# Neighbourhood attention with stacked query halves, three score buffers, and turning ahead of the last values

## The reference, cut to what matters

```python
def dense_attention(q, k, v):
    s = jnp.einsum('bqhd,bkhd->bhqk', q, k).astype(jnp.float32) * (q.shape[-1] ** -0.5)
    p = jax.nn.softmax(s, axis=-1).astype(v.dtype)
    return jnp.einsum('bhqk,bkhd->bqhd', p, v)

def neighbourhood_attention(q, k, v, k_ctx, v_ctx, rpb, rows):
    ...
    s_loc = jnp.einsum('brqhd,brikhd->bhrqik', qg, k_band).astype(jnp.float32) * scale + bias.astype(jnp.float32)
    s_loc = jnp.where(in_win[:, None, :], s_loc, -jnp.inf)
    s_loc = s_loc.reshape(bsz, h, rows, GRID_W, wr * GRID_W)
    s_ctx = jnp.einsum('brqhd,blhd->bhrql', qg, k_ctx).astype(jnp.float32) * scale
    p = jax.nn.softmax(jnp.concatenate([s_loc, s_ctx], axis=-1), axis=-1).astype(v.dtype)
    ...
    o = jnp.einsum('bhrqik,brikhd->brqhd', p_loc, v_band) + jnp.einsum('bhrql,blhd->brqhd', p_ctx, v_ctx)
    return o.reshape(bsz, n, h * dh)

def diff_attend(q1, q2, k1, k2, v, lam):
    ...
    p = jax.nn.softmax(s1, axis=-1) - lam * jax.nn.softmax(s2, axis=-1)
    return jnp.einsum('bhqk,bkhd->bqhd', p.astype(v.dtype), v)
```

## Time and profile before

| | |
|---|---|
| median of 3 runs | 2925.27 us (2922.05 to 2929.17) |
| the profiled execution | 2929.45 us, of which the span is 2927.6 us |
| TensorE matmul busy | 2836.5 us, 97% of the span |
| VectorE busy | 1750.9 us, 60% |
| ScalarE busy | 990.6 us, 34% |
| mean granted TensorE clock | 0.988 of full speed |

### The profile page before, as it was taken

One profiled execution on the slowest core, in us unless ns is written; L12 is line 12 of the kernel. 1 busy time (PEld: TensorE's weight loads), 2 busy tenths in 40 slices (PEclk: granted clock), 3 DMA queues, 4 the chain that ended last, 5 costly groups with the idle time before them and its releaser, 6 DMA issues.

```text
span 2927.6 us, 37226 instructions
## 1 busy us (share of the span) xinstructions
PE 2836.5 (97%) x15519; PEld 2435.8 (83%) x15519; DVE 1750.9 (60%) x2406; ACT 990.6 (34%) x1371; POOL 121.5 (4%) x157
## 2 busy tenths in 40 slices
PE   6999999999999999999989999999999988999999
PEld 5888887979788888789878888888888987888887
DVE  6656655555567777566486565655555348454454
ACT  4333333232333222332275232222213237432222
POOL 0100000000001100000000000000000000000000
PEclk9999999999999999999989999999999999999999
DMA  7343344545234644333600212333322151222232
GB/s 248 121 139 108 119 153 149 175 119 168 92 117 141 179 144 146 97 123 101 144 30 16 86 58 87 94 105 92 99 65 92 61 116 39 64 85 89 93 108 72
DMA packets 267507, 317.17 MB, mean 108 GB/s; under 512 B 24859, under 2 KB 236203, under 8 KB 267340
## 3 DMA queue, kind: packets, MB, share of 16 engines
q1 hardware_dynamic: 240764, 230.60, 25.8%
q0 software_dynamic: 19456, 72.00, 8.3%
q10 hardware_dynamic: 7120, 12.20, 1.3%
HBM read 291.96 MB, written 11.27 MB: 104 GB/s over the span
## 4 chain that ended last, share of the span: by engine, by line
PE 89%; DVE 5%; ACT 2%; DVEq 2%; issue 1%; DMA 0%; ACTq 0%
PE psum L625 26%; PE psum L627 26%; PE psum L626 26%; PE psum L1068 2%; PE psum L855 1%; PE psum L1080 1%; DVE dneg L2473 1%; DVE sba L2484 1%; DVE n_t L1921 1%; PE psum L842 1%; ACT pt L1738 1%; PE psum L928 1%; DVE w_lo L1933 1%; PE psum L1159 1%; PE psum L1149 0%
## 5 line engine op out<-in xcount | busy, mean ns | idle before, releaser
L625 PE MATMUL psum<-hs_hi,w_hi 128*128 128x512 f32 x1632 | 647.2, 397 | 10.4 <-DVE hs_lo L1925 7.6
L1933 DVE TENSOR_TENSOR w_lo<-raw,w_hi 128x2048 fp32r<-128x2048 f32 (+1 forms) x246 | 435.7, 1771 | 357.8 <-ACT w_hi L1301 245.7
L626 PE MATMUL psum<-hs_hi,w_lo 128*128 128x512 f32 x1632 | 637.3, 391 | 0.0
L627 PE MATMUL psum<-hs_lo,w_hi 128*128 128x512 f32 x1632 | 637.3, 390 | 0.0
L625 PEld LDWEIGHTS psum<-hs_hi,w_hi 128*128 128x128 f32 x1632 | 307.6, 188 | 84.5 <-issue 10.2
L627 PEld LDWEIGHTS psum<-hs_lo,w_hi 128*128 128x128 f32 x1632 | 307.2, 188 | 65.1
L626 PEld LDWEIGHTS psum<-hs_hi,w_lo 128*128 128x128 f32 x1632 | 307.7, 189 | 61.3 <-issue 1.0
L1993 DVE SCALAR_TENSOR_TENSOR ada_acc<-ada_raw,csil,ada_acc 128x512 f32<-128x512 f32 x392 | 279.7, 749 | 38.0 <-DMA ada_raw<-in_w_ada 19.8
L1311 ACT CAST w_hi<-raw 128x2048 fp32r<-128x2048 f32 (+1 forms) x138 | 191.3, 1386 | 325.7 <-PE psum L627 313.8
L625 PE MATMUL psum<-mid_hi,w_hi 128*128 128x512 f32 x768 | 300.7, 392 | 0.0
L626 PE MATMUL psum<-mid_hi,w_lo 128*128 128x512 f32 x768 | 299.1, 389 | 0.0
(11 more groups left out here) (361 smaller groups left out, 4534.2 us busy)
## 6 DMA issues: line engine op xcount, KB each, us to landing
raw<-in_w_in SPq DMA_DIRECT2D x56, 1024.0 KB, 5.2
ada_raw<-in_ada_w POOLq DMA_DIRECT2D x96, 512.0 KB, 4.0
raw<-in_w_ff SPq DMA_DIRECT2D x48, 1024.0 KB, 5.5
raw<-in_w_ff SPq DMA_DIRECT2D x96, 512.0 KB, 3.4
ada_raw<-in_w_ada POOLq DMA_DIRECT2D x32, 512.0 KB, 4.1
raw<-in_w_in SPq DMA_DIRECT2D x24, 512.0 KB, 4.6
raw<-in_w_ret_out SPq DMA_DIRECT2D x16, 512.0 KB, 3.4
raw<-in_w_out SPq DMA_DIRECT2D x8, 1024.0 KB, 5.0
```

The costliest lines, as they stand in the source:

```text
L625: pe.matmul(dst, lhi, rhi, start=start, stop=False)
L626: pe.matmul(dst, llo, rhi, start=False, stop=False)
L627: return pe.matmul(dst, lhi, rlo, start=False, stop=stop)
L1933: low = dve.tensor_tensor(w_lo[par][:, k0:kt], raw[par][:, k0:kt], w_hi[par][:, k0:kt].bitcast(F32), ALU.subtract)
```

## The change

**Scores by two products.** A head fills only half of the 128 rows, so the queries' high half now lies in one half of `naqs` and the low half in the other, and the keys' high half stands twice, one above the other (`naks_hi`), as does the low half (`naks_lo`). One matmul against `naks_hi` gives high by high plus low by high; a second against `naks_lo` gives high by low plus low by low. The stacked keys are made by 16 DMAs from SBUF to SBUF in each layer.

**Buffers.** Three score buffers of two banks (`SPAIR`) in place of two of three, four buffers of exponentials (`sba`, `sbb`), two of turned tiles (`pt2`).

**Orders.** The two attentions get a TensorE loop of their own, and the copy of a full item's turned tiles is split into tiles 4 and 5, then 0 to 3. Some jobs of ScalarE and VectorE move from the end of the differential loop into it.

```diff
+                def stack_keys(tokens, context, src, src_c, made):
+                    for dst_of, whole, j in ((tokens, src, 1), (context, src_c, 2)):
+                        sp.wait_ge(made, 2 * l + j)
+                        for a in range(2):
+                            for half in range(2):
+                                sp.dma_start(dst_of(a)[HD * half:HD * (half + 1)].bitcast(F32),
+                                             whole[HD * a:HD * (a + 1)].bitcast(F32)).then_inc(nk_stacked, 16)
+                stack_keys(lambda a: naks_hi[:, a:4:2, :], lambda a: nakcs_hi[:, a:4:2, :], nak_hi, nakc_hi, nk_hi)
+                stack_keys(lambda a: naks_lo[:, a:4:2, :], lambda a: nakcs_lo[a], nak_lo, nakc_lo, nk_split)
                 sp.wait_ge(df_s, 24 if l == 0 else 40)
...
+            def diff_attention(l, score, free, next_score):
...
                     if i + 2 < len(its):
                         score(i + 2, its[i + 2])
+                    elif i < len(its):
+                        next_score(i + 2 - len(its))
...
+            def na_attention(l, score):
...
+                t0 = turn_groups(att_items(0)[0], 24) * l
+                score(2, its[2])
+                for i in range(len(its) + 1):
+                    if i < len(its):
+                        it = its[i]
+                        pe.wait_ge(na_exp, i0 + i + 1)
+                        if i == 0:
+                            pe.wait_ge(df_out, g0 + its[-1].group + 1)
+                            pe.wait_ge(df_pt, i0 + len(its))
+                        else:
+                            pe.wait_ge(na_pt, t0 + turn_groups(its, i))
+                        if it.pos == 1 and it.group and not it.ctx:
+                            pe.wait_ge(na_out, g0 + it.group)
+                        for tiles in ([range(2)] if it.ctx else [range(4, 6), range(4)]):
+                            for t in tiles:
+                                mm = pe.transpose(T2[:, t * P:(t + 1) * P], sbn[i % 4][:, t * P:(t + 1) * P], ident[:])
+                            mm.then_inc(na_t, 1)
+                    if i:
+                        last = its[i - 1]
+                        pe.wait_ge(na_pt, t0 + turn_groups(its, i) + (1 if i < len(its) and not its[i].ctx else 0))
+                        if last.pos == 0 and last.group:
+                            pe.wait_ge(na_out, g0 + last.group)
+                        item_values(last, pt2[(i - 1) % 2], nav).then_inc(na_pv, 1)
+                    if i + 3 < len(its):
+                        score(i + 3, its[i + 3])
...
                 def na_score(i, it):
...
+                    dst = SPAIR[i % 3]
...
+                    if i == 0:
+                        pe.wait_ge(nk_stacked, 256 * (l + 1))
+                    if i < 3:
+                        pe.wait_ge(df_e2, i0 + len(its) - (1 if i == 0 else 0))
                     else:
+                        pe.wait_ge(na_exp, i0 + i - 2)
...
+                        pe.matmul(dst[:, 0:S], q_, naks_hi[:, it.head, :], start=True, stop=False)
+                        pe.matmul(dst[:, 0:S], q_, naks_lo[:, it.head, :], start=False, stop=True)
                     a_ = 0 if it.ctx else S
+                    pe.matmul(dst[:, a_:a_ + SC], q_, nakcs_hi[:, it.head, :], start=True, stop=False)
+                    pe.matmul(dst[:, a_:a_ + SC], q_, nakcs_lo[it.head % 2][:, it.head // 2, :], start=False, stop=True).then_inc(na_s, 1)
...
+                def na_take_pt(i, it):
+                    if i >= 2:
+                        act.wait_ge(na_pv, i0 + i - 1)
+                    elif i == 0:
+                        act.wait_ge(df_pv, i0 + N_)
+                    for j, (t_, n_) in enumerate([(0, 2)] if it.ctx else [(4, 2), (0, 4)]):
+                        act.wait_ge(na_t, t0 + turn_groups(its, i) + j + 1)
+                        turned(i % 2, t_, n_).then_inc(na_pt, 1)
...
-                    if 4 <= i < 8:
-                        odd = i % 2
-                        z = (qz_hi if i < 6 else qz_lo)[odd][HD * (1 - odd):HD * (2 - odd)]
-                        act.activation(z, zero_c(HD * (1 - odd)), ACT.Copy, scale=0.0)
-                    if i == N_ - 4:
+                    if i == N_ - 9:
                         act.copy(nak_hi[:], nak[:]).then_inc(nk_hi, 1)
...
+                    elif i == N_ - 8:
                         act.copy(nakc_hi[:], nakc[:]).then_inc(nk_hi, 1)
+                    elif i == N_ - 6:
+                        nq_his(first_of[0])
...
                 na_exps(0, its[0])
+                na_exps(1, its[1])
                 for i in range(N_):
-                    if i + 1 < N_:
-                        na_exps(i + 1, its[i + 1])
+                    if i + 2 < N_:
+                        na_exps(i + 2, its[i + 2])
...
-                    take_pt(i, its[i], na_t, na_pt, na_pv)
+                    na_take_pt(i, its[i])
...
+                    if i == N_ - 8:
+                        key_los(1, nak_lo, nak, nak_hi)
+                    elif i == N_ - 7:
+                        key_los(2, nakc_lo, nakc, nakc_hi)
+                    elif i == N_ - 5:
+                        nq_los(first_of[0])
+                    elif i == N_ - 4:
+                        dve.wait_ge(bb_in, 128 * (l + 1))
+                        mask_bias(0)
...
+                na_max(0, its[0])
                 df_take(its[-1])
                 na_max(1, its[1])
+                na_max(2, its[2])
...
-                    if i + 2 < N_:
-
-                        if its[i + 2].pos == 0 and not its[i + 2].ctx:
-                            mask_bias(its[i + 2].head)
-                        dve.wait_ge(na_exp, i0 + i + 1)
-                        na_max(i + 2, its[i + 2])
+                    if i + 3 < N_:
+
+                        if its[i + 3].pos == 0 and not its[i + 3].ctx:
+                            mask_bias(its[i + 3].head)
+                        na_max(i + 3, its[i + 3])
```

More of the change, by code:

```diff
@@ L150, in att_items, with turn_groups @@
     return its, 24 * l, 8 * l
+def turn_groups(its, i):
+    return sum(1 if it.ctx else 2 for it in its[:i])
 def build(nc, d, out):
@@ L1047, in _, with item_values @@
             feed_forward(FU["ff"], 0, 2, 0, (hs_ready, lambda k: 8 + k + 1), None, "", ahead=context_tiles, twin=True)
-            def attention(l, kind, sems, score, values, free, last_copied):
-                done_t, pt_ok, p_ok, pv, outs = sems
+            def item_values(it, pt_, values):
+                nt = it.keys // P
+                for t in range(nt):
+                    mm = pe.matmul(O2[:, it.pos * HD:(it.pos + 1) * HD], pt_[:, t, :],
+                                   values[:, t + 6 - nt, it.head * HD:(it.head + 1) * HD], start=t == 0, stop=t == nt - 1)
+                return mm
+            def diff_attention(l, score, free, next_score):
                 its, i0, g0 = att_items(l)
@@ L1192, in _ @@
                 its = att_items(l)[0]
-                groups = its[-1].group + 1
                 def df_free(it):
@@ L1199, in df_free @@
                         pe.wait_ge(df_out, g0 + it.group)
-                def na_free(it):
-                    pe.wait_ge(df_out, g0 + groups)
-                    if g0 + it.group:
-                        pe.wait_ge(na_out, g0 + it.group)
-                attention(l, "diff", (df_t, df_pt, df_comb, df_pv, df_out), df_score, dfv, df_free, lambda: None)
                 def na_score(i, it):
-                    c = it.head // 2
                     tok = slice(it.tile * P, (it.tile + 1) * P)
-                    dst = S3[i % 2]
+                    dst = SPAIR[i % 3]
@@ L1227, in _ @@
+                diff_attention(l, df_score, df_free, lambda i: na_score(i, its[i]))
+                na_attention(l, na_score)
                 y0 = 12 * l
@@ L1783, in na_exps @@
-                    if it.pos == 0 and it.group > 1:
-                        act.wait_ge(na_out, g0 + it.group - 1)
-                    act.activation(sba[i % 2][:, 0:it.keys], S3[i % 2][:, 0:it.keys], ACT.Exp, bias=stat2[:, i % 2:i % 2 + 1],
-                                   accum_out=den[:, it.group % 2, it.pos:it.pos + 1]).then_inc(na_exp, 1)
+                    if i >= 4:
+                        act.wait_ge(na_t, t0 + turn_groups(its, i - 3))
+                    if it.pos == 0 and it.group > 3:
+                        act.wait_ge(na_out, g0 + it.group - 3)
```

145 lines of the change are left out of this document (66 added, 79 removed).

## The result

The changed kernel takes 3030.87 us (median of 6 runs, 3025.86 to 3040.03) against 2928.29 us for the kernel before (median of 6 runs). The ratio is 1.036, with an interval of 1.034 to 1.037: 3.6% slower. The forecast of 3006 us has the direction and the cause. It is 25 us short. The largest part of that is one term of the sum, the clock; the jobs moved into the differential loop are the second.

The account below looks back on a forecast made before the run. TensorE was taken to bound the kernel before, a closed ring the changed loop. 2929.45 us + 58 (26 + 24 + 6 + 2) + 23 for the clock = 3010, less 4.2 to the median: 3006 us; range 2976 to 3041.

Parts of the forecast that it names:

- The closed ring (part 2): Neighbourhood loop: values wait behind a newer item's score, maximum and exponential; one item per turn, 5.58 us against 3.11.
- Start and end (parts 3 and 4): Neighbourhood stretches: first values 8.0 us after the last differential values; whole stretches +24 us in layer 0, +26 in layer 1.
- The clock (part 7): Neighbourhood loop: TensorE's clock goes to and fro, 40% at the half clock, 23 us more.
- The sum: Whole kernel: 2929.45 us profiled + 58 at the full clock + 23 for the clock = 3010 us.
- the half clock throughout: Rival: TensorE stays at 1.2 GHz in the neighbourhood stretches, 58 us for the clock, 3041 us; chance 0.15.
- the likeliest case: Mixture of full and half clock in the neighbourhood stretches, 2992 to 3024 us; chance 0.56.
- Part 1: Neighbourhood scores: two products for three remove TensorE work, 11.5 us over full items and 1 us over context items.
- the rival of an open ring: Neighbourhood loop: ScalarE's first copy precedes the wait for the exponential, period 2.75 us, 2913 us in all; chance 0.05.
- The moved jobs (part 5): Differential loop: key and query low halves and first mask, moved inside on nearly full VectorE, cost 3 us per layer.
- The stacking (part 6): Before neighbourhood score 0: TensorE waits for 16 stacking DMAs, 2 us in layer 0, no cost in layer 1.
- Full clock all along: Rival: waits of 2.6 us don't lower TensorE's clock in the neighbourhood stretches, 2983 us; chance 0.22.

Follow-up runs that it names:

- the gap filled: Changed kernel plus nine extra 512-column matmuls with unread results per turn of full items, between turning item i and values of item i-1: 2990.26 us, 1.0195.
- both open: Changed kernel with ScalarE copying item i before the exponential of i+2, and TensorE issuing score i+3 before the values of i-1: 2925.08 us, 0.9992.

## Why the prediction was right, and where it wasn't

**The closed ring (part 2).** Right, in its place and its size. The deciding order on ScalarE is shown by moving it alone. The turn was put at 5.58 us at the full clock and 7.16 at the half; the runs show 5.42 and 7.32. The chain of the earlier trace rows and the short copy of the earlier trace rows carried over as read.

**Start and end (parts 3 and 4).** The first values of layer 1 start at 2523.80, 7.6 us after the last differential values (2516.23); I had 8.0. With the gap filled the stretches are 95.8 and 87.8 us, for 95.2 and 82.3. In layer 0 that is right. In layer 1 the values of item 12 start at 2568.83, 74.9 us after the last differential values, where I had 75. Only what follows is longer, 12.9 us for 7.3, and that is the part without filling, at a granted clock of 0.50. So the count holds, and these 5.6 us are the clock's.

**The clock (part 7).** This is the term that was mis-sized. A turn at the half clock was put at 1.6 us more, and 1.9 were measured. The share was not right: I put it at 40%, the rows show 80%. The sum had 23 us for the clock; against full-clock stretches of 95.8 and 82.2 us (87.8 less those 5.6) the two neighbourhood stretches after (115.4 and 101.8) show 39. That is less than 80% of the 58 us put down for the half clock throughout (46); about 20 of those 58, for starts, ends and context items, came from no row. The 47 us of the ratios agree with either within their interval. I argued that 5.2 us without a gap had to bring the clock back, from 3.98 of 4 busy in the earlier trace rows. It did bring it back, but only in some turns (2 of 10 successive ones of layer 1), and hardly for longer than the values. In three stretches of 8 us each of layer 1, after:

```profile
2548.00:2556.00 8.00, 5.73 (x24) 4.89 (x22) 4.09 (x7) 1.74 (x4) 0.00 (x0) 0.50 0.00 0
2556.00:2564.00 8.00, 5.49 (x22) 4.90 (x22) 4.22 (x7) 3.29 (x6) 3.98 (x3) 0.55 0.01 2
2564.00:2572.00 8.00, 5.46 (x30) 4.96 (x30) 2.24 (x4) 2.89 (x8) 0.00 (x0) 0.66 0.00 0
```

The values of 2564.71 took 1.55 us; the 256-key products behind them, at 2566.64, already took 0.41 again. I should have counted not only whether the clock returns but how much of a turn is left once it has. Nor does a stretch without a gap bring it back each time: from 2500 to 2512 us, in layer 1's differential loop after, TensorE is busy for 12.00 of 12 us and the granted clock is 0.50 all through; the last 12.9 us of the gap-filled kernel's layer 1 look the same. The rival of the half clock throughout (3041 us) was nearer than the likeliest case. The page "TensorE: Matmul & The Clock Gate" of the Trainium skill, section "A second HAM failure mode: psum-queue depth-cycling", describes a clock that swings when TensorE pauses briefly between groups of matmuls; the trace agrees with the swing (1.55 and 2.82 us for the same values).

**What else was short.** The profiled execution is 29.6 us above the sum of 3010. The clock in the two neighbourhood stretches makes 16 of that (39 for 23), the differential stretches 7.6 (15.6 for the 8 of parts 5 and 6), and 5.0 lie outside the four stretches. The ring, start and end at the full clock came out as summed (51 for 50).

**Part 1.** The 12.5 us of TensorE work had been priced as worth their time where TensorE is the bound. They are worth nothing in either loop. It didn't touch the forecast, because the ring was closed, but it is the reason why the rival of an open ring (2913 us) was too low: with ScalarE's order open the kernel takes 2931 us, with both open 2925. Its period was put at 2.75 us, TensorE's work; VectorE's load and hand-overs don't let it get there. The sentence "TensorE is the bound" was read off an engine without a wait. Two paths of 3.1 us ran side by side there, and only an item without score products told them apart.

**The moved jobs (part 5).** Right in kind, too small in layer 1: 9.5 us for 3, with about 1.9 us for the two neighbourhood scores that now lie there. Timeline, end of layer 1's differential loop, after:

```profile
2497.69 1.08 DVE L2575 TENSOR_TENSOR na_bias<-na_bias,na_mask 128x896 f32<-128x896 f32 x1
...
2499.09 0.42 DVE L2552 TENSOR_TENSOR y_diff<-psum,rden 128x256 f32<-128x256 f32 x1
...
2499.66 0.66 PE L1100 MATMUL psum<-ident,sba 128*128 128x128 f32 x2 [2.85 <-DVE y_diff L2552]
```

The mask costs more than its 1.08 us, as it stands ahead of the division that frees `O2`: TensorE, which can't turn its last two tiles before that, idles 2.85 us, and then works at the half clock from 2500 to 2512 us. The same wait was 0.82 us in the kernel before, with the full clock behind it. Another such wait, of 1.57 us behind a key low half, ends at 2481.65 (0.37 before), with the same fall behind it. I had priced the instructions and not what waits behind them. In layer 0 the differential stretch grew by 6.1 us, where I had 5 for parts 5 and 6. Taking the jobs out of the loop gave 4 to 7 us back in layer 1.

**The stacking (part 6).** Right: in front of neighbourhood score 0 TensorE waits in layer 0 and not in layer 1. Layer 0, after:

```profile
1529.50 0.77 PE L1263 MATMUL psum<-naks_hi,naqs 128*128 128x512 f32 x1 [2.18 <-issue]
```

I had taken 2 us. The profile names no releaser for this wait; in the kernel that stacks the keys at the start of the loop it is gone.

**The other rivals.** Full clock all along (2983 us) is what the gap-filled kernel comes to, 2990 us, and only because something filled the gap.

## What to carry to other kernels

An engine without a single wait may still not be the bound: look for an item in which part of its work is missing (the last ones of a loop), and see whether the period changes. When a software pipeline is reordered, walk one iteration through every in-order queue and ask which instruction of an older item stands behind one of a younger item; if the answers close into a circle, its whole latency is paid once per item, however many buffers there are. And price a job that moves into a full loop by who waits behind it, and by the clock that the wait may cost, not by its own duration.

## What the runs showed of the hardware

**Idle time on TensorE cost nearly twice its length here.** A turn of the ring takes 2.3 us more than an item before (5.42 us for 3.11) at the full clock, and another 1.9 us (7.32) at the half clock that came with its gaps. Nine matmuls per turn that compute nothing returned 1.6% of the kernel's time.

**The clock isn't decided by the nearest gaps alone.** Before layer 1's differential attention both kernels run the same instructions with the same waits. The kernel before:

```profile
2375.27 3.79 PE L1149 MATMUL psum<-sgu,wst 128*128 128x64 f32 x32 [0.68 <-ACT wst L1717]
```

The changed kernel:

```profile
2427.38 4.69 PE L1199 MATMUL psum<-sgu,wst 128*128 128x64 f32 x32 [0.68 <-ACT wst L1761]
```

In the 8 us up to this point TensorE is busy for 6.56 us in both, but in the 8 us that follow the granted clock is 1.00 in the one and 0.63 in the other. These 32 matmuls take 3.79 us in four of the twelve kernels (the one before, its version with two products, and the two that open the ring at one engine alone) and 4.6 us or more in the other eight, though none of the edits touches the instructions ahead of them. In layer 0, ahead of the first differential score, the same line's 48 matmuls behind the same two waits (0.77 and 0.68 us) take 5.57 us in five of the twelve kernels and 8.88 to 9.59 in the other seven, and with the matmuls behind them the difference is 4.9 to 6.6 us. The kernel before, the changed one and the one with the gap filled are among the seven; the one that opens the ring at ScalarE and the one with both orders are among the five, so about 5 us of what their profiles show against the kernel before lies here. Differences of up to 6.6 us in layer 0 and of 3 to 4 in layer 1 stand between these profiles by nothing that was changed there. Whether they belong to a kernel or to the one execution of it that was profiled, and what decides them, stays open.
